# Latent attention: four heads in a block for the first two tiles of queries, with heads four apart side by side

## What is computed

```python
def mla_attend(q_lat, q_rope, rows, mask):
    ckv = rows[..., :MLA_KV_RANK]
    kr = rows[..., MLA_KV_RANK:]
    s = (jnp.einsum('bqhc,bkc->bhqk', q_lat, ckv) + jnp.einsum('bqhr,bkr->bhqk', q_rope, kr)).astype(jnp.float32)
    s = jnp.where(mask, s * ((MLA_NOPE + MLA_ROPE) ** -0.5), NEG_INF)
    p = jax.nn.softmax(s, axis=-1).astype(rows.dtype)
    return jnp.einsum('bhqk,bkc->bqhc', p, ckv)
```

## Time and profile before

| | |
|---|---|
| median of 3 executions | 1073.14 us (1069.68 to 1076.78) |
| the profiled execution | 1069.19 us |
| its span, first to last instruction | 1067.5 us |
| mean granted TensorE clock | 0.949 |
| busy share PE, PEld, DVE, ACT, POOL | 91%, 56%, 49%, 33%, 23% |
| instructions | 17835 |

### The profile page before, as it was taken

The page is one execution under the profiler, slowest core; times in us unless marked ns, Lnnn a source line. Parts: engine busy times, 40 slices in busy tenths (PEclk is TensorE's granted clock), DMA queues, the critical chain, the costliest instruction groups (busy, mean ns, idle before and its releaser), DMA issues.

```text
span 1067.5 us, 17835 instructions
## 1 busy us (share of the span) xinstructions
PE 967.2 (91%) x6998; PEld 595.7 (56%) x6998; DVE 526.6 (49%) x1078; ACT 353.7 (33%) x881; POOL 249.6 (23%) x276
## 2 busy tenths in 40 slices
PE   7978999998999998899999398999899887999995
PEld 6866788887445857633333156657548663333332
DVE  0245630366748657333223465684178584333327
ACT  2325432020001523233333354554214332333423
POOL 2220620042501002355410005500000015352121
PEclk9998999999999998999999699899999976999998
DMA  9431460172206253989999603441146146999978
GB/s 324 112 92 31 105 200 9 71 198 79 69 0 154 77 210 131 402 325 410 411 404 354 231 1 78 97 135 62 55 144 276 40 158 205 342 396 408 417 226 196
DMA packets 81611, 203.72 MB, mean 191 GB/s; under 512 B 22682, under 2 KB 47938, under 8 KB 72432
## 3 DMA queue, kind: packets, MB, share of 16 engines
q1 hardware_dynamic: 61568, 153.44, 39.6%
q0 software_dynamic: 19952, 49.05, 14.8%
HBM read 184.46 MB, written 25.92 MB: 197 GB/s over the span
## 4 chain that ended last, share of the span: by engine, by line
PE 77%; DVE 10%; DMA 4%; ACT 4%; issue 2%; POOL 0%; SPq 0%; DVEq 0%; POOLq 0%; ACTq 0%
PE PS L1614 15%; PE PS L1417 11%; PE PS L1055 9%; PE PS L1156 6%; PE PS L1631 6%; PE PS L1440 3%; PE PS L1120 3%; PE PS L1764 2%; ACT arena L1995 2%; DMA x<-y_tok 2%; PE PS L1078 2%; PE PS L1598 2%; PE PS L1043 2%; PE PS L1839 2%; PE PS L1849 2%
## 5 line engine op out<-in xcount | busy, mean ns | idle before, releaser
L1995 ACT ACTIVATE arena<-PS 32x520 f32<-32x520 f32 (+9 forms) x150 | 73.7, 503 | 185.0 <-PE PS L1055 43.6
L1614 PE MATMUL PS<-ring,arena 128*32 128x512 f32 x648 | 116.9, 592 | 1.4 <-DVE arena L3057 1.4
L1614 PE MATMUL PS<-arena 128*32 128x512 f32 x648 | 112.7, 611 | 3.0 <-issue 2.0
L1055 PE MATMUL PS<-xT,ring 128*128 128x260 f32 x416 | 95.0, 389 | 3.8 <-DVE arena L2485 2.3
L3073 DVE COPY arena<-PS 128x256 f32<-128x256 f32 x24 | 10.2, 425 | 171.6 <-PE PS L1622 171.6
L1055 PEld LDWEIGHTS PS<-xT,ring 128*128 128x128 f32 x416 | 79.4, 193 | 18.8 <-DVE arena L2485 4.3
L2279 ACT ACTIVATE arena<-PS,lnc 128x128 f32<-128x128 f32 x184 | 66.8, 469 | 33.9 <-PE PS L1598 33.8
L1631 PE MATMUL PS<-ring,arena 128*32 128x512 f32 x432 | 69.0, 595 | 1.2 <-DVE arena L3073 1.2
L826 POOL TENSOR_TENSOR rstd<-rstd,small 128x1 f32<-128x1 f32 (+1 forms) x20 | 12.6, 628 | 244.3 <-DVE rstd L2773 244.3
L1156 PE MATMUL PS<-ring,xT 128*128 128x256 f32 (+2 forms) x336 | 65.1, 354 | 0.0
L1614 PEld LDWEIGHTS PS<-arena 128*32 128x32 f32 x648 | 30.1, 113 | 60.8 <-issue 56.5
(11 more groups left out here) (440 smaller groups left out, 1861.5 us busy)
## 6 DMA issues: line engine op xcount, KB each, us to landing
arena<-in_moe_w_in_dram SPq DMA_DIRECT2D x27, 1024.0 KB, 10.3
ring<-in_moe_w_in_dram SPq DMA_DIRECT2D x27, 1024.0 KB, 12.9
ring<-in_moe_w_out_dram SPq DMA_DIRECT2D x18, 1024.0 KB, 11.5
ring<-in_w_in_even_dram SPq DMA_DIRECT2D x11, 1024.0 KB, 12.0
xT<-in_moe_w_in_dram SPq DMA_DIRECT2D x10, 1024.0 KB, 11.8
arena<-in_moe_w_out_dram SPq DMA_DIRECT2D x8, 1024.0 KB, 13.6
xT<-in_moe_w_out_dram SPq DMA_DIRECT2D x6, 1024.0 KB, 15.0
y_tok<-in_c_zeros_dram POOLq DMA_DIRECT2D x8, 512.0 KB, 11.0
```

The source lines that it names most:

```text
L1055: mm = pe.matmul(o[out_rows, 512 * h:512 * h + HALF], lhs(k), rhs(k)[:, HALF * h:HALF * h + HALF], start=(k == 0), stop=(k == nk - 1))
L1614: mm = pe.matmul(o[group(q), 0:512], xT_[:, k, group(q)], w(q, k), start=(k == 0), stop=(k == KD - 1), **quarter(q))
L1995: return act.activation(dst, src, ACT.Copy)
```

## The change

Tiles 0 and 1 get blocks of four heads, tiles 2 and 3 keep two. There are then 2+2+4+4 = 12 blocks in place of 16, and 36 jobs in place of 48. Since 12 jobs fewer is a multiple of four, and four blocks fewer is a multiple of two, all later jobs keep their PSUM pairs and their buffers. In a block of four a head has 256 columns, so two heads share a bank: the block takes heads 0, 4, 1, 5 (or 2, 6, 3, 7) and computes the scores of its first and third, then of its second and fourth, so that two heads whose rotary matmuls follow each other still lie in different banks and in different rows of the array. The copy of the outputs puts the heads back in place. The ten passes over `x` now begin after block 3, and the last two both come after block 11.

```diff
-MLA_BLOCKS = [(n, h, 2, 128 * (n + 1)) for n in range(4) for h in range(0, 8, 2)]
+MLA_HEADS_AT_ONCE = (4, 4, 2, 2)
+MLA_BLOCKS = [(n, h, g, 128 * (n + 1)) for n, g in enumerate(MLA_HEADS_AT_ONCE) for h in range(0, 8, g)]
...
+def latent_heads(h0, g):
+
+    return [h0, h0 + 1] if g == 2 else [h0 // 2 + b + 4 * a for b in range(2) for a in range(2)]
...
-GAIN_BLOCKS = 6
+GAIN_STEPS = {3: [0], 4: [1], 5: [2], 6: [3], 7: [4], 8: [5], 9: [6], 10: [7], 11: [8, 9]}
...
-                    for h in range(h0, h0 + g):
-                        pe.matmul(o[:, h - h0, 0:w], q_lat[:, h, n * P:n * P + P], ckvT[:, 0:w], start=True, stop=False)
-                    for h in range(h0, h0 + g):
-                        b, c = 32 * (h % 4), h // 4
-                        mm = pe.matmul(o[:, h - h0, 0:w], qrT2[b:b + 32, c, n * P:n * P + P], krT4[b:b + 32, 0:w],
-                                       start=False, stop=True, **({"tile_position": (b, 0)} if b == 96 else {}))
+                    heads = list(enumerate(latent_heads(h0, g)))
+
+                    for pair_ in (heads[0::2], heads[1::2]) if g == 4 else (heads,):
+                        for j, h in pair_:
+                            pe.matmul(o[:, j, 0:w], q_lat[:, h, n * P:n * P + P], ckvT[:, 0:w], start=True, stop=False)
+                        for j, h in pair_:
+                            b, c = 32 * (h % 4), h // 4
+                            mm = pe.matmul(o[:, j, 0:w], qrT2[b:b + 32, c, n * P:n * P + P], krT4[b:b + 32, 0:w],
+                                           start=False, stop=True, **({"tile_position": (b, 0)} if b == 96 else {}))
...
-                        take(att_key(kind, "O", i), ctxT[:, h0:h0 + g, tile_cols(n)],
-                             lambda o: o[:, 0:g * P].rearrange("p (g q) -> p g q", g=g))
+                        dst = ctxT[:, h0:h0 + g, tile_cols(n)]
+                        if g == 4:
+                            dst = ctxT[:, :, tile_cols(n)].rearrange("p (a b) q -> p b a q", a=2)[:, h0 // 2:h0 // 2 + 2, :, :]
+                            take(att_key(kind, "O", i), dst, lambda o: o[:, 0:g * P].rearrange("p (b a q) -> p b a q", b=2, a=2))
+                        else:
+                            take(att_key(kind, "O", i), dst, lambda o: o[:, 0:g * P].rearrange("p (g q) -> p g q", g=g))
...
-                    if i == GAIN_BLOCKS:
-                        dve.wait_ge(s["ln_in"], 32 * 3)
-                    if i >= GAIN_BLOCKS:
-                        t, c = divmod(i - GAIN_BLOCKS, 2)
+                    for step in GAIN_STEPS.get(i, []):
+                        if step == 0:
+                            dve.wait_ge(s["ln_in"], 32 * 3)
+                        t, c = divmod(step, 2)
```

## The result

The changed kernel takes 1078.07 us, the median of 20 executions (1070.86 to 1086.44). The kernel before takes 1071.20 us, the median of 20 (1069.30 to 1079.86). The ratio is 1.0056, 95% interval 1.0037 to 1.0076, so about 6 us slower. I had forecast 1073.3 us and a range up to 1077.0; the median lies 1.1 us above it.

What follows compares the result with a forecast made beforehand. The stage was taken as bound by what PE streams. Joints -0.24, a removed wait -0.22 and a new wait +0.67 gave +0.2 us on 1073.14, so 1073.3 us, range 1068.5 to 1077.0.

Steps and rivals of the forecast that it cites:

- Joints: On PE, four merged pairs of transpose jobs each save a start-up of 0.06 us: 0.24 us saved.
- T2's wait: In tile 1, PE's transposes of block 2 wait once on the longer exponentials of four heads: +0.67 us.
- the fill at the start: The first transposes wait for scaling on DVE, some 3.0 us, covered by 3.32 us of scores: no wait, at either clock.
- The chain behind T2: In tile 1, from the end of block 3's scores through mask, maxima and scaling to the end of exponentials: 4.26 us.
- So PE's streaming is as before, at zero gain or loss: In the latent attention stage, PE's matmuls and transposes stream the same columns after the change: 0 us.
- If the clock stays low longer: Listed sign that the prediction is wrong: the low clock at tile 0 lasting longer than before; no size given.
- A slow PE gives the other engines time: nothing waits there: In tile 0, at half clock for 6.83 us, PE has no waits on other engines.
- Rival A: If low clock misses tile 0, the kernel before waits 0.9 and 0.4 us at its first transposes; 1.3 faster, chance 0.18.
- Rival D: The new 0.67 us gap in tile 1 brings another low-clock stretch: 1.7 to 3.4 us slower, chance 0.08.
- Rivals B and C: B: PE follows DVE and ACT, 3.9 us faster, chance 0.04; C: longer exponential chains starve PE, 2.7 slower, 0.10.

Runs made afterwards that it cites:

- e2: The kernel before plus eleven extra matmuls on 128 rows in PE's two idle stretches just ahead of the first scores: 1071.02 us, ratio 0.9972.
- e1: The changed kernel plus eleven extra matmuls on 128 rows in PE's two idle stretches just ahead of the first scores: 1068.17 us, ratio 0.9942.
- e5: The changed kernel plus eleven extra matmuls in the same two idle stretches, but on 32 rows of the array: 1075.12 us, ratio 1.0014 to the kernel before.
- e11: The changed kernel, nothing altered, profiled a third time: low stretch 27.31 us, stage 71.14 us.
- e9: The changed kernel, nothing altered, profiled a second time: low stretch 6.83 us, stage 62.83 us.

## Why the prediction was wrong, step by step

- **Joints, T2's wait and the fill at the start: right.** T2 waited 0.65 us (forecast 0.67), the mask on 512 elements took 0.70 and the maxima on 1024 1.22 us, there was no wait at T0, T1 and O0. DVE ended its passes with 5.47 idle us to spare. By these alone the change is near zero, and with the clock up even a gain of 0.7 us. The chain behind T2 was forecast 0.1 us too long (4.26 against 4.16).
- **The step that failed** is "So PE's streaming is as before, at zero gain or loss". The columns that PE streams are as before; the clock at which it streams them is not. I took the low stretch of 6.83 us as a given of both kernels, and asked what PE's slowness does to the other engines and not what the new order of PE's work does to the clock. The sum has no term for a longer low stretch. It should have had one: in the changed kernel 6.83 us more of it cost 3.2 us (66.00 against 62.83), and in the first pair of profiles this is nearly the whole of the 3.7 us. "If the clock stays low longer" stands among the signs of being wrong, and that is what came; but no chance and no term went with it.
- **What was right and not drawn on:** "A slow PE gives the other engines time: nothing waits there". It also means that the small jobs of the kernel before cost little while the clock is low, so that the change had little to gain there.
- **The starting point.** The forecast was +0.2 us on 1073.14, the median of three executions; the median of 20 is 1071.20. Against that the error is 6.7 us and not 4.8.
- **Rival A: its mechanism was right**, with 0.81 + 0.31 us in e2. Its count from the rows is 1.83 - 1.06 = 0.77 and 1.83 - 1.34 = 0.49 us; the text has 0.9 and 0.4, with nearly the same sum. It gains only when the clock is up near S0, and none of the six profiles of the two unfilled kernels had that.
- **Rival D had nearly the right price (3.4 us) and the wrong cause.** I tied a further low stretch to the gap of 0.67 us at T2. That gap came 6 us after the clock was back, and brought nothing. The loss was in the stretch that existed already. That a low stretch costs half of its length was too much for the kernel before, where 6.83 us cost 1.8 (62.34 against 60.53).
- **Rivals B and C fell.** In the stage, the saved DVE and ACT instructions gave at most the 0.7 us of e1 against e2, and no second T job of the merged blocks or behind them waited on their exponentials.
- **The range** had its upper end from rival D, and that was priced by the one low stretch I had seen, 6.83 us long, in an execution of 1069.19 us. Two later profiles of the same kernel had 13.65 us, and one of the changed kernel 27.31.

## What to carry to other kernels

Ahead of a stage that starts after a pause of TensorE, look at the granted clock, and at what PE then works on. Merging blocks puts more scores, and so more matmuls that use only part of the array's rows, ahead of the first transposes, and here a stage with the same columns to stream was at half clock for longer. Where the profile shows a pause of a few microseconds in which PE waits for another engine, matmuls on all rows whose results are thrown away can cost nothing and keep the clock: here eleven of them turned a loss of 0.6% into a gain of 0.6% against the kernel before. Try them on both kernels, for half of that gain (0.3%) came in the kernel before as well.

A waiting time that a slow clock covers is not gone. Take the profile's clock as one draw: read two or three profiles of the same kernel before a term of a few microseconds is put at zero.

## What the runs showed of the hardware that I had not expected

- TensorE with an instruction at every moment still dropped to half clock: in e5 it was busy 3.68 of 3.68 us ahead of S0, nearly all of it with matmuls on 32 rows and 8 rows, and fell to 0.50 at 674.50. The same instructions on 128 rows (e1) kept it at 1.00. Over all executions the mean granted clocks are 0.9447 and 0.9522.
- At half clock it stayed there through 13.65 us (first profile of the changed kernel) and 27.31 us (e11) of work in which PE was busy all the time or all but 1 us.
- The low stretch near S0 of the same program differed from 6.83 to 27.31 us between executions (e9 and e11). Of the 17.4 us by which their spans differ (1067.9 and 1085.3), 8.3 lie in the stage; the other 9.1 lie in the rest of the program.
